# When a fused two-network kernel loads its first expert weights

## The reference

```python
for l in range(2):
    h = x * (1 + scale1) + shift1
    x = layer_norm(ALPHA * x + gate1 * token_mixer(h), ln1_g[l], ln1_b[l])
    h = x * (1 + scale2) + shift2
    x = layer_norm(ALPHA * x + gate2 * moe_ffn(h), ln2_g[l], ln2_b[l])

def moe_ffn(h):            # 8 of 64 experts per token, and one shared expert
    scores = sigmoid(h @ router_w)
    eidx, wts = top_k(...)  # 4 of 8 groups, then 8 experts
    routed = sum over e of wts * ((silu(h @ w_gate[e]) * (h @ w_up[e])) @ w_down[e])
    return routed + (silu(h @ ws_gate) * (h @ ws_up)) @ ws_down
```

## Time and profile before

| | us |
|---|---|
| median of 3 runs | 3000.25 |
| lowest and highest | 2990.05, 3000.75 |
| profiled execution | 2994.28 |
| its span, first to last instruction | 2992.5 |
| PE busy | 2798.5 (94%) |
| DVE busy | 1629.0 (54%) |
| ACT busy | 756.6 (25%) |
| bytes moved | 718.31 MB, mean 240 GB/s |

### The profile page before, as it was taken

One profiled execution on the slowest core, in us unless ns is written; L12 is line 12 of the kernel. 1 busy time (PEld: TensorE's weight loads), 2 busy tenths in 40 slices (PEclk: granted clock), 3 DMA queues, 4 the chain that ended last, 5 costly groups with the idle time before them and its releaser, 6 DMA issues.

```text
span 2992.5 us, 65346 instructions
## 1 busy us (share of the span) xinstructions
PE 2798.5 (94%) x27418; PEld 2077.7 (69%) x27418; DVE 1629.0 (54%) x2821; ACT 756.6 (25%) x1400; POOL 409.8 (14%) x343
## 2 busy tenths in 40 slices
PE   7999999988899999999989899999998999899998
PEld 6878566655587866655557588844577887888973
DVE  6745433333473554444436478788757536555555
ACT  0122212121112133323213422200045414443210
POOL 1000000000000000000000036400014302434630
PEclk9999999999999999999999999999999999999999
DMA  9945999999984599999974035485430023000443
GB/s 392 389 161 219 406 405 415 386 421 420 389 365 141 205 381 420 419 407 420 420 310 141 15 113 171 168 308 197 154 106 18 4 82 129 18 16 33 157 167 112
DMA packets 102704, 718.31 MB, mean 240 GB/s; under 512 B 11680, under 2 KB 11968, under 8 KB 18176
## 3 DMA queue, kind: packets, MB, share of 16 engines
q1 hardware_dynamic: 98448, 700.02, 59.5%
q0 software_dynamic: 3952, 14.00, 1.5%
HBM read 711.09 MB, written 2.88 MB: 239 GB/s over the span
## 4 chain that ended last, share of the span: by engine, by line
PE 74%; DVE 12%; DMA 9%; ACT 2%; issue 2%; SPq 0%; POOL 0%; DVEq 0%; ACTq 0%; POOLq 0%
PE ps L229 16%; PE ps L1614 10%; PE ps L2167 9%; PE ps L2192 7%; DMA arena<-in_w_up 6%; DVE arena L162 6%; PE ps L3139 5%; PE ps L1643 5%; PE ps L2832 3%; PE ps L1705 2%; ACT arena L145 2%; DMA arena<-in_w_down 2%; DVE arena L166 2%; PE ps L2559 1%; PE ps L3571 1%
## 5 line engine op out<-in xcount | busy, mean ns | idle before, releaser
L145 ACT ACTIVATE arena<-ps 128x512 f32<-128x512 f32 (+3 forms) x529 | 266.9, 505 | 1268.0 <-PE ps L229 244.7
L229 PE MATMUL ps<-arena 128*128 128x256 f32 x2144 | 480.1, 385 | 18.5 <-DMA arena<-in_w_in 4.9
L162 POOL TENSOR_TENSOR arena<-arena 128x512 f32<-128x512 f32 (+1 forms) x288 | 376.4, 1307 | 821.7 <-DVE arena L162 284.4
L229 PEld LDWEIGHTS ps<-arena 128*128 128x128 f32 x2144 | 408.7, 192 | 87.1 <-issue 9.7
L1614 PE MATMUL ps<-arena 128*32 128x256 f32 (+2 forms) x5120 | 390.8, 389 | 42.0 <-DMA arena<-in_w_up 31.0
L1614 PEld LDWEIGHTS ps<-arena 128*32 128x32 f32 (+2 forms) x5120 | 248.5, 120 | 187.4 <-issue 87.8
L162 DVE TENSOR_TENSOR arena<-ps,arena 128x256 f32<-128x256 f32 (+3 forms) x416 | 203.8, 490 | 235.0 <-PE ps L3139 87.9
L162 DVE TENSOR_TENSOR arena<-arena 128x512 f32<-128x512 f32 (+6 forms) x473 | 294.1, 622 | 60.7 <-PE ps L2192 35.7
L2167 PE MATMUL ps<-arena 128*128 128x256 f32 (+1 forms) x1792 | 298.5, 328 | 2.2 <-DVE arena L162 1.5
L2192 PE MATMUL ps<-arena 128*128 128x512 f32 x672 | 293.0, 593 | 2.4 <-DVE arena L162 2.2
L2167 PEld LDWEIGHTS ps<-arena 128*128 128x128 f32 x1792 | 270.0, 191 | 29.6 <-DVE arena L171 3.3
(11 more groups left out here) (278 smaller groups left out, 2912.1 us busy)
## 6 DMA issues: line engine op xcount, KB each, us to landing
arena<-in_w_gate SPq DMA_DIRECT2D x128, 1024.0 KB, 13.0
arena<-in_w_up SPq DMA_DIRECT2D x128, 1024.0 KB, 14.1
arena<-in_w_down SPq DMA_DIRECT2D x128, 1024.0 KB, 13.5
arena<-in_mlp SPq DMA_DIRECT2D x80, 1024.0 KB, 4.8
arena<-in_w_ada SPq DMA_DIRECT2D x48, 1024.0 KB, 13.1
arena<-in_ada SPq DMA_DIRECT2D x48, 1024.0 KB, 4.9
arena<-in_w_in SPq DMA_DIRECT2D x30, 1024.0 KB, 11.3
arena<-in_w_rkv SPq DMA_DIRECT2D x20, 1024.0 KB, 4.9
```

What stands on the lines that cost most here:

```text
L145: self.e.activation(out, in_, func, bias=bias, scale=scale, **more).then_inc(*self.done(key))
L162: self.e.tensor_tensor(out, a, b, op).then_inc(*self.done(key))
L229: ins = pe.matmul(out, a, b, start=start and i == 0, stop=stop and i == len(pairs) - 1)
```

## The change

The shared gate and the first six expert weights (gates and ups of round 0, gates of round 1, `FRONT`) are issued in `mixer_sp` behind w_out 0, into slots 5 to 11, of which 9 to 11 wait for the mixer's last probabilities. For that the mixer's memory is laid out anew, so that what slots 9 to 11 cover (`hT`, `PP`, `PT`, `qT`) is dead by then. The ring of the expert part starts at slot 0, and `fresh` goes. The context comes later: in layer 0 its rows are loaded behind the gates of round 4, with a wait for gate 1, and normed at the end of step 3, and its pieces stand in later rounds; in layer 1 what was kept is loaded behind the gates of round 2, and the rows wait for gate 1; the first two heads are a round later. Mixer 1 waits for "c kept" on ACT and DVE.

```diff
+        def load_apart(sp, i, key, used, src):
+            turn, weights.turn, size, weights.size = weights.turn, i, weights.size, len(tiles)
+            load(sp, key, used, src)
+            weights.turn, weights.size = turn, size
...
+                (self.yT, self.PQt, self.sg, self.tabs, self.lg, self.lb, self.PQ, self.TM, self.sbv, self.GS, self.Z, self.kT,
+                 self.oaT, self.obT, self.gain, self.ws) = carve(
+                    0, 2048, 1280, 512, 256, 1024, 1024, 1536, 1536, 512, 4096, 2048, 512, 1024, 1024, 640, 1024,
+                    end=ARENA - NEXTRA * 2048)
+                self.hT, self.PP, self.PT, self.qT = carve(
+                    ARENA - NEXTRA * 2048, 2048, 8 * 256, 2 * 512, 1024, end=ARENA - (NAHEAD + 1) * 2048)
...
+        FRONT = [(name, r, e) for name, r in (("w_gate", 0), ("w_up", 0), ("w_gate", 1)) for e in places_of(r)]
...
-            for i in range(4):
+            load(sp, ("w_out", l, 0), ("mixed", l, 0, 1), D["w_out"][l, 0])
+            for i in range(NRING + NAPART, NRING + NEXTRA):
+                weights.used[i] = [(("mixer", l), "values", 3, 0)]
+            load_apart(sp, NRING, ("ws_gate", l), ("shared gate", l), D["ws_gate"][l])
+            for i, (name, r, e) in enumerate(FRONT):
+                load_apart(sp, NRING + 1 + i, (name, l, e), (name[2:], l, r), expert_rows(sp, name, l, e))
+            for i in range(1, 4):
                 load(sp, ("w_out", l, i), ("mixed", l, i, 1), D["w_out"][l, i])
...
-        PIECE_ROUNDS = {1: [("rows", 0), ("rows", 1), ("rows", 2)], 2: [("rows", 3), ("qkv", 4)], 3: [("keys", 0), ("keys", 1)],
-                        6: [("qkv", 5)], 7: [("qkv", 0)], 9: [("queries", 0)], 10: [("qkv", 1)], 12: [("queries", 1)], 15: [("qkv", 2)],
-                        16: [("queries", 2)], 17: [("qkv", 3)], 18: [("queries", 3)]}
+        PIECE_ROUNDS = {4: [("rows", 0), ("rows", 1), ("rows", 2)], 5: [("rows", 3), ("qkv", 4)], 6: [("keys", 0), ("keys", 1)],
+                        8: [("qkv", 5)], 9: [("qkv", 0)], 10: [("queries", 0)], 12: [("qkv", 1)], 13: [("queries", 1)],
+                        15: [("qkv", 2)], 16: [("queries", 2)], 17: [("qkv", 3)], 18: [("queries", 3)]}
...
-        for a, p in enumerate((1, 3, 7, 10, 14, 16, 18, 21)):
-            q = {3: 6, 7: 9, 10: 12}.get(p, p + 1)
+        for a, p in enumerate((2, 4, 7, 10, 14, 16, 18, 21)):
+            q = {4: 6, 7: 9, 10: 12}.get(p, p + 1)
...
-            weights.size, weights.turn, weights.fresh = NRING + EXTRA[l], NRING, ("mixer", l)
-            load(sp, ("ws_gate", l), ("shared gate", l), D["ws_gate"][l])
+            weights.size, weights.turn = NRING + EXTRA[l], 0
             for p, new, _, _ in rounds(l):
                 if new == 2:
                     ended(sp, ("mixer", l), "pe", "act", "dve")
...
-                if new is not None:
+                if new is not None and new > 1:
                     for e in places_of(new):
                         load(sp, ("w_gate", l, e), ("gate", l, new), expert_rows(sp, "w_gate", l, e))
+                if new == 2 and l:
+                    sp.wait_ge(*at["c kept"])
+                    sp.dma_start(gates[:, 0:1024], kept[:, 2048:3072]).then_inc(*tables["rows"](None, 16))
+                    sp.wait_ge(*at["scores", l])
+                    sp.dma_start(rw, kept[:, 3072:3584]).then_inc(*tables["rows"]("c values kept", 16))
+                    sp.wait_ge(*at["gate", l, 1])
+                    sp.dma_start(CX.rows, kept[:, 0:2048]).then_inc(*tables["rows"]("c queries kept", 16))
+                if new == 4 and not l:
+                    sp.wait_ge(*at["gate", l, 1])
+                    sp.dma_start(CX.rv, D["ctx"].rearrange("(t p) n -> p t n", p=128)).then_inc(*tables["rows"]("rows", 16))
...
+                if p == 3 and not l:
+                    act.wait_ge(*at["gate", l, 1])
+                    context_rows_act(act, do)
...
-                if p < 0 and not l:
+                if p == 3 and not l:
                     context_rows_dve(dve, do)
```

More of the change, by code:

```diff
@@ L318, in load @@
                 sp.wait_ge(*at[use])
-            if i >= NRING + NAPART and weights.fresh is not None:
-                ended(sp, weights.fresh, "pe", "act", "dve")
-                weights.fresh = None
             dst = tile[:, 0:src.shape[1]] if parts is None else tile.rearrange("p (a b) -> p a b", a=parts)
             sp.dma_start(dst, src).then_inc(*weights.landed[i](key, 16))
+        def load_apart(sp, i, key, used, src):
+            turn, weights.turn, size, weights.size = weights.turn, i, weights.size, len(tiles)
+            load(sp, key, used, src)
+            weights.turn, weights.size = turn, size
         def freed(pe, old):
@@ L876, in program @@
         M = MixerMemory()
+        FRONT = [(name, r, e) for name, r in (("w_gate", 0), ("w_up", 0), ("w_gate", 1)) for e in places_of(r)]
+        assert len(FRONT) == NEXTRA - 1
         def mixer_heads(l):
@@ L1033, in mixer_act @@
                 ended(act, ("moe", l - 1), "pe", "dve")
+                act.wait_ge(*at["c kept"])
             act.wait_ge(*mods(0, l, 0, 1))
@@ L1061, in mixer_dve @@
                 ended(dve, ("moe", l - 1), "pe", "act")
+                dve.wait_ge(*at["c kept"])
             else:
@@ L1470, in moe_sp @@
                     ended(sp, ("mixer", l), "pe", "act", "dve")
[L1471 to L1476, removed]
                     sp.wait_ge(*at["ids", l])
-                    if l:
-                        sp.wait_ge(*at["scores", l])
-                        sp.dma_start(rw, kept[:, 3072:3584]).then_inc(*tables["rows"]("c values kept", 16))
-                if new is not None:
+                if new is not None and new > 1:
                     for e in places_of(new):
                         load(sp, ("w_gate", l, e), ("gate", l, new), expert_rows(sp, "w_gate", l, e))
+                if new == 2 and l:
[8 more added lines that the diff above has]
+                    sp.dma_start(CX.rv, D["ctx"].rearrange("(t p) n -> p t n", p=128)).then_inc(*tables["rows"]("rows", 16))
                 early_sp(sp, l, p, (0,))
@@ L1487, in moe_sp @@
                         load(sp, ("w_down", l, e), ("yd", l, p, 1), expert_rows(sp, "w_down", l, e))
-                if new is not None:
+                if new:
                     for e in places_of(new):
@@ L1748, in moe_act @@
                 gather(0, k)
-            if not l:
-                context_rows_act(act, do)
             for p, new, Q, ks in rounds(l):
```

## The result

| | before | after |
|---|---|---|
| median of 8 runs each on one chip, us | 2993.93 | 3006.94 |
| lowest and highest | 2989.35, 3000.75 | 3002.40, 3012.37 |
| profiled execution, its span | 2994.28, 2992.5 | 3003.29, 3001.5 |
| expert part 0 in it | 501.3 | 512.6 |
| from there to part 1 (mixer 1) | 263.6 | 259.3 |

A forecast was written before the change was run, and what follows sets the result against it. It took TensorE and full DMA queues in the two MoE blocks as the bound. Block 0's 10.5 plus block 1's 6.8 gave +17.3 us: 3011.6 for the profiled execution, 3017 for a median, range 2992 to 3028.

The forecast's parts named there:

- Early loads, 0: Seven expert weights issued earlier in each mixer: effect 0, since the ids come no sooner and nobody waits for them.
- The two slots more at the ids: At the ids, 12 resident weights against 10 (11 in block 1): value 0, bounds -2 to 0 us.
- Part 0, 10.5: Block 0's expert part: 7 + 2.5 + 1 = 10.5 us longer, bounds 1.2 and 14.5.
- The starved stream: Block 0, rounds 5 to 7: late PE starves the DMA stream, up 12 waits; +7 us, bounds 0.7 and 9.4.
- Behind the hole: Block 0, 549 to 640 us, after the DMA gap at 537 to 549: PE 7.8 later, stream loses 1 us (0 to 2.6).
- The added megabyte: Block 0's context, 1 MB, now in the full stream behind gate 4: +2.5 us, paid at the hole at 537.
- The reserve: Loads issued in 411 to 422 us: issue to landing 6.7 against 4.8 on an idle queue, only 1.9 us spare.
- the queue absorbs it: Rival: in-flight loads cover PE's late rounds; block 0 pays 2.5 + 0.7, block 1 about 5: +8, 3008 us; chance 0.28.
- The stall, 1.8 to 2: Block 0, first row job of round 4: PE waits for the context's norm 1.8, taken as 2 us, bounds 0 to 3.6.
- Part 1, 6.8: Block 1's expert part: kept data's bytes 3.7 plus DMA hole 3.1, 6.8 us longer; bounds 3.7 and 9.
- that only the two parts count: The sum took only block 0's 10.5 and block 1's 6.8, 17.3 us, with no term for later stages.
- The lead kept: Rival: loads stay two ahead in each block and PE's early rounds are lighter; 2983 to 2990 us; chance 0.12.

The follow-up runs named there:

- mended order: Kernel after, with layer 1's kept data behind gates of round 3, row jobs in later seats, qkv in rounds 7, 9, 10, 16, 18, 20; against before 1.0003, again 1.0008.
- the last experiment: Kernel before, with one added wait: GpSimd's second piece of last-MLP sums waits until VectorE added read-out rows; 2989.25 against 2992.17 us, ratio 0.9992.

## Why the prediction was nearly right, and where it was off
**Early loads, 0: right.** Shown by themselves, +2 (-2 to +6). The two slots more at the ids gave nothing either.

**Part 0, 10.5: the mechanism right, the size a little high.** The two traces give 11.3, the means 8.9. The starved stream was 7 in the forecast; the stages lose 4.9 + 3.1 = 8.0, and up 12 is 6.6 late (6.0 counted from round 0). Behind the hole 1 was forecast, 2.4 measured. The added megabyte, 2.5, was not measured by itself in this part. The reserve read off the landing times (6.7 - 4.8 = 1.9 us) was the number that decided, and "the queue absorbs it" fell as a description of part 0: the stream of 411 to 450 lost 53 GB/s. The mended order, which takes the qkv jobs out of steps 5 and 8, has 402 GB/s there and part 0 of before to about 1 us by the mean. So the added megabyte doesn't show as a full term of 2.5 there; but part 0 of before alone differs by 4.9 between executions, so how much of it is hidden is open.

**The stall, 1.8 to 2: undersized, and mostly without effect.** It measured 2.97, because VectorE's own operations of round 4 stand behind the scalings; up to their end it would have been 1.3. Taken away from the transposes it came back as a wait of 1.89 for the same VectorE, and the part changed by less than executions differ.

**Part 1, 6.8: right, 6.6 by the means,** of which 3.3 went with the hole and 3.3 stayed as bytes. From the gates of round 2 to the end of gate 1 it is 1061.0 to 1075.1, 14.1 us, where the forecast had 13.8, and the rows go out at 1075.2. The heads one round later brought waits of PE for ACT that the prediction doesn't name (2.25 and 1.10 us at 1108.8 and 1129.2); that they add nothing to the part is argued from the sum and not tested. The forecast's own terms for the rows, 1067.8 + 0.4 + 2.3, make 1070.5 and not 1070.3, 0.2 us more of hole.

**The step that failed: that only the two parts count.** The sum ended with the second expert part. It took the ring for a queue of the experts alone (it now starts at slot 0) and did not ask which slot the next user gets. The ring's turn behind part 1 decides which weights of the last stages wait for which, and that gave back 4.9 us (85.6 against 80.7), by an accident that has nothing to do with the change's purpose. With it the forecast would have been 17.3 - 4.9 = 12.4 us, against 12.6 measured. That they meet so closely is luck: the means of the parts give 8.9 + 6.6 - 4.9 = 10.6, inside the interval of 9 to 16.5. So the total of "the queue absorbs it" (8) lies nearly as close as the forecast's, though its reason fell.

**The lead kept** (2983 to 2990) fell: the ids came no sooner, up 3 began at 339.5 as before, and down 3 waited 5.8 us. The mended order pays some 4 us in the parts (the kept data's bytes) and takes 3.3 or 4.9 back at the end (82.3 and 80.7); against before it is a draw, and no kernel here beats before for certain.

## What to carry to other kernels
A load that is issued earlier is worth what waits for it: look at the stage where the engine idles, and find out whether the queue is held by data or by a value that must be computed first. Room in a full stream is read from the time between issue and landing, less that of a load on an idle queue: here work of PE that was shifted by more than this (8.9 us against 1.9) starved it, and the loss was kept. And a ring that begins one slot further on shifts who waits for whom in every later stage that shares it, so a comparison of the total should be split by stages before it is put down to the edit.

## What was not expected of the hardware
VectorE and GpSimd at once: while GpSimd ran 128x512 float32 sums of 1.3 to 1.4 us each, VectorE's operations out of SBUF took 1.17 instead of 0.35 (scaling of 128x128), 1.51 instead of 0.42 (sum of two 128x256) and 1.70 instead of 0.69 (sum of two 128x512), 0.8 to 1.1 us more each; the one that reads one operand from PSUM and one from SBUF kept its 0.74 for two (2771.88 in the last experiment, with GpSimd at work until 2776.2). The Trainium skill (SBUF — State Buffer, SBUF: two separate sides) says that a VectorE operation with two SBUF inputs (beside a GpSimd operation that reads SBUF), or in a mode that takes two ports, and a GpSimd operation shut each other out for a whole instruction, whichever starts first, and that other VectorE operations don't wait. The sums and the operation on PSUM agree, the waits being less than one of GpSimd's operations; that the scaling ran in such a mode no row shows.

PE after a wait: the group behind a wait of 2.2 to 5.8 us often takes 5.35 or more instead of 3.66 (521.05 and 1116.36 in the kernel after), and 3.66 behind 1.2: for a part of it PE ran at the lower of its two clocks, 1.2 instead of 2.4 GHz, and the granted clock is 0.59 in 521.0 to 527.3 and 0.69 in 1116.3 to 1121.8. But behind the 2.84 at 339.51 it took 3.66 at a clock of 1.00, so a wait's second cost can't be told from its length here.
